# Down projection: nine seven-product tiles in both column pairs, their sums regrouped, two loads moved

## The reference, cut to what matters

```python
def _swiglu(x, w_gate, w_up, w_down):
    return (jax.nn.silu(x @ w_gate) * (x @ w_up)) @ w_down

def reference(x, ...):
    m = _dsa_mixer(x, *mix_p)
    x = _layer_norm(alpha * x + m, ln1_g, ln1_b)
    x = _layer_norm(alpha * x + _swiglu(x, w_gate, w_up, w_down), ln2_g, ln2_b)
    return x
```

## Time and profile before

| | us |
|---|---|
| median of three runs | 916.3 (916.14 to 917.05) |
| the profiled execution | 916.54 |
| its span, first to last instruction | 914.8 |
| outside the span | 1.7 |
| PE busy | 908.9 |
| DVE busy | 774.6 |
| ACT busy | 548.7 |
| POOL busy | 154.3 |

### The profile page before, as it was taken

One profiled execution on the slowest core, in us unless ns is written; L12 is line 12 of the kernel. 1 busy time (PEld: TensorE's weight loads), 2 busy tenths in 40 slices (PEclk: granted clock), 3 DMA queues, 4 the chain that ended last, 5 costly groups with the idle time before them and its releaser, 6 DMA issues.

```text
span 914.8 us, 11657 instructions
## 1 busy us (share of the span) xinstructions
PE 908.9 (99%) x4340; PEld 761.4 (83%) x4340; DVE 774.6 (85%) x963; ACT 548.7 (60%) x748; POOL 154.3 (17%) x119
## 2 busy tenths in 40 slices
PE   9999999999999999999999999999999999999997
PEld 8999988888888888888888888888888888888885
DVE  6778566578799899999999899999989998998677
ACT  5686765345356667666757666675756565466450
POOL 0205540001531214031421214010060000000000
PEclk9999999999999999999999999999999999999999
DMA  9743423574959696969879697978488747365642
GB/s 359 321 177 139 139 92 136 193 312 150 378 165 264 219 310 191 345 182 306 220 250 285 231 317 189 326 206 277 150 306 297 282 184 272 124 247 185 230 138 92
DMA packets 63239, 210.08 MB, mean 230 GB/s; under 512 B 5584, under 2 KB 11728, under 8 KB 51920
## 3 DMA queue, kind: packets, MB, share of 16 engines
q1 hardware_dynamic: 57712, 198.86, 60.6%
q0 software_dynamic: 5472, 10.49, 6.8%
HBM read 199.36 MB, written 9.96 MB: 229 GB/s over the span
## 4 chain that ended last, share of the span: by engine, by line
PE 99%; DVE 0%; ACT 0%; DVEq 0%; issue 0%; ACTq 0%
PE acc L2226 20%; PE acc L2199 18%; PE acc L2181 12%; PE acc L1969 10%; PE tp L2181 9%; PE tp L2199 6%; PE acc L1907 5%; PE tp L2226 5%; PE acc L1828 4%; PE acc L2106 2%; PE tp L2144 2%; PE acc L1941 1%; PE tp L2020 1%; PE tp L1955 1%; PE tp L2033 1%; PE tp L1817 0%
## 5 line engine op out<-in xcount | busy, mean ns | idle before, releaser
L1153 ACT ACTIVATE w_hi<-raw 128x512 fp32r<-128x512 f32 (+1 forms) x164 | 117.7, 761 | 90.9 <-PE acc L2226 70.7
L1576 DVE TENSOR_TENSOR w_lo<-raw,w_hi 128x512 fp32r<-128x512 f32 (+1 forms) x164 | 136.7, 863 | 24.7 <-ACT w_hi L1153 24.1
L2226 PE MATMUL acc<-w_hi,hid_t 128*128 128x512 f32 x480 | 155.5, 389 | 0.0
L2199 PE MATMUL acc<-w_hi,act_t 128*128 128x512 f32 x480 | 154.3, 391 | 0.0
L1507 DVE TENSOR_TENSOR w_lo<-raw,w_hi 128x1024 fp32r<-128x1024 f32 x83 | 104.1, 1256 | 5.4 <-ACT w_hi L1095 5.3
L2199 PEld LDWEIGHTS acc<-w_hi,act_t 128*128 128x128 f32 x480 | 90.1, 188 | 20.7 <-issue 2.1
L1082 ACT ACTIVATE w_hi<-raw_b 128x1024 fp32r<-128x1024 f32 x70 | 74.2, 1060 | 54.2 <-PE acc L2199 31.5
L2226 PEld LDWEIGHTS acc<-w_hi,hid_t 128*128 128x128 f32 x480 | 90.1, 188 | 18.8
L1082 ACT ACTIVATE w_hi<-raw 128x1024 fp32r<-128x1024 f32 x63 | 66.6, 1058 | 48.5 <-PE acc L2199 33.5
L1501 DVE TENSOR_TENSOR w_lo<-raw_b,w_hi 128x1024 fp32r<-128x1024 f32 x70 | 86.9, 1242 | 10.0 <-ACT w_hi L1082 10.0
L2226 PE MATMUL acc<-w_lo,hid_t 128*128 128x512 f32 x240 | 93.4, 389 | 0.0
(11 more groups left out here) (294 smaller groups left out, 1939.8 us busy)
## 6 DMA issues: line engine op xcount, KB each, us to landing
raw<-in_w_pairs SPq DMA_DIRECT2D x116, 512.0 KB, 6.3
raw<-in_w_down SPq DMA_DIRECT2D x44, 1024.0 KB, 5.7
raw_b<-in_w_pairs SPq DMA_DIRECT2D x40, 512.0 KB, 8.0
raw<-in_w_out SPq DMA_DIRECT2D x16, 1024.0 KB, 4.9
raw<-in_w_gu SPq DMA_DIRECT2D x8, 1024.0 KB, 11.4
raw<-in_x_w SPq DMA_DIRECT2D x14, 552.0 KB, 7.4
hid_blocks<-local SPq DMA_DIRECT2D x11, 512.0 KB, 8.5
turned<-hid_blocks SPq DMA_DIRECT2D x44, 128.0 KB, 4.3
```

The lines of the kernel that those rows point to most:

```text
L1153: act.activation(unit_parts(u)[0], block_of(b, block, width), ACT.Copy).then_inc(down_hi_done, 1)
L1576: dve.tensor_tensor(lo_, block_of(b, block, width), hi_, ALU.subtract).then_inc(down_lo_done, 1)
L2199: last = pe.matmul(out[:, t, :], act_t[:, k0 + m, x, t * P:(t + 1) * P], part[:, cols][:, m * GC:(m + 1) * GC], start=False, stop=(end and ...
L2226: last = pe.matmul(bank, lhs(x), part[:, cols * GC:(cols + 1) * GC], start=(first == u and (cols, x) == (0, 0) and part is hi_), stop=(end ...
```

## The change

Both pairs get nine quads. A quad's seven products are put into four units: W1 (blocks B11 and B21, two products, two blocks wide), W2 (t1 and B22, two products, two wide), T2 (t2, one product, one wide) and W3 (t3 and t4, two products, two wide). The order is W1, in most quads a plain unit, W2, a plain unit, T2, W3. The sum t1 is made by an accumulating DMA that POOL issues (`add_down`); t2 is made by DVE right after the low part of W2, and t3 and t4 after the low part of the unit behind W2. A quad's slot is loaded in two transfers of 512 KB, first the half with B12 and B22, which t1 waits for. There are still four slots; a slot is now given to the load whose predecessor ends first (`down_places`). The load of `x1` moves behind the load of slot 9, that of the norm rows behind the load of slot 36; slot 5 comes after `blocks_store`, and slot 6 after `blocks_load`. The low part of the second late tile moves from POOL to DVE (`LATE_LOW`).

```diff
-QUADS_OF = (len(DOWN_QUADS), EARLY_QUADS)
-REST = ((18, 19), (20, 21)), ((14, 15), (16, 17), (18, 19), (20, 21))
+QUAD_UNITS = ((B11, 2, (S_A11, S_A12)), (B12, 2, (S_S1, S_S4)), (B12, 1, (S_S2,)), (B11, 2, (S_S3, S_A22)))
+QUADS_OF = (len(DOWN_QUADS), len(DOWN_QUADS))
+LEAD = ((1,), ())
+BETWEEN = ((3, 5, 7, 9, 11, 13, 15, 17), (1, 3, 5, 7, 9, 11, 13))
+REST = ((18, 19), (20, 21)), ((15, 17), (18, 19), (20, 21))
...
+        extra = len(halves) - quads
+        doubled = {n * quads // extra for n in range(extra)}
+        for q in range(quads):
+            w1, w2, t2, w3 = [(DOWN_QUADS[q], ("quad", q, m)) for m in range(len(QUAD_UNITS))]
+            steps += [w1] + ([halves.pop(0)] if q in doubled else []) + [w2, halves.pop(0), t2, w3]
...
-LAST_TURN = 8
-LAST_HID = 28
-LATE_HIGH = 4
+LAST_TURN = 5
+LAST_HID = 17
+LATE_HIGH = 8
+LATE_LOW = 10
...
+def down_places():
+    held, place, prior = {}, [], []
+    for b in range(len(DOWN_SLOTS)):
+        if b < DOWN_PLACES:
+            at = (b + 2) % RING
+        else:
+            at = min(range(RING), key=lambda n: SLOT_LAST[held[n]])
...
 (load_down)
-                    sp.wait_ge(down_lo_done, SLOT_LAST[b - RING] + 1)
-                sp.dma_start(raw[:, down_slot(b), :], a["w_down"][b]).then_inc(raw_full[down_slot(b)], 16)
+                    sp.wait_ge(down_lo_done, SLOT_LAST[DOWN_PRIOR[b]] + 1)
+                n, src = DOWN_PLACE[b], a["w_down"][b]
+                if b in QUAD_SLOTS:
+                    sp.dma_start(block_of(b, B12, 2), src[:, B12 * GC:(B12 + 2) * GC]).then_inc(right_full_d[n], 16)
+                    sp.dma_start(block_of(b, B11, 2), src[:, B11 * GC:(B11 + 2) * GC]).then_inc(down_full[n], 16)
+                else:
+                    sp.dma_start(block_of(b, 0, 4), src).then_inc(down_full[n], 16)
...
 (the SP queue)
-            sp.wait_ge(ffn_full, TILES)
-            sp.wait_ge(x1_stored, 16)
-            sp.dma_start(x1[:], x1_rows).then_inc(x1_back, 16)
-            for b in range(RING, RING + 2):
+            load_down(RING)
+            blocks_store(PAIRS - 1)
+            load_down(RING + 1)
+            blocks_load(PAIRS - 1)
+            for b in range(RING + 2, len(DOWN_SLOTS)):
                 load_down(b)
-            blocks_store(PAIRS - 1)
-            for b in range(RING + 2, 2 * RING):
-                load_down(b)
-            blocks_load(PAIRS - 1)
-            rows(ln2_rows, 2, ln2_rows_full)
-            for b in range(2 * RING, len(DOWN_SLOTS)):
-                load_down(b)
+                if b == X1_BEHIND:
+                    sp.wait_ge(ffn_full, TILES)
+                    sp.wait_ge(x1_stored, 16)
+                    sp.dma_start(x1[:], x1_rows).then_inc(x1_back, 16)
+                if b == ROWS_BEHIND:
+                    rows(ln2_rows, 2, ln2_rows_full)
...
 (DVE)
+            def quad_t2(u):
+                b = DOWN_UNITS[u][1]
+                dve.wait_ge(down_lo_done, u + 1)
+                dve.tensor_tensor(block_of(b, B12), block_of(b, B12), block_of(b, B22), ALU.add).then_inc(t_done, 1)
+
+            def quad_t34(u):
+                b = DOWN_UNITS[u][1]
+                b11, b21, t2 = (block_of(b, n) for n in (B11, B21, B12))
+                dve.wait_ge(t_done, quad_sums(u) + 1)
+                dve.tensor_tensor(b11, t2, b11, ALU.subtract).then_inc(t_done, 1)
+                dve.tensor_tensor(b21, t2, b21, ALU.add).then_inc(t_done, 1)
...
 (POOL)
+            def add_down(b):
+                n = DOWN_PLACE[b]
+                pool.wait_ge(right_full_d[n], 16 * quad_fill(b))
+                pool.dma_start(block_of(b, B12), a["w_down"][b][:, B11 * GC:(B11 + 1) * GC],
+                               accum_op=ALU.add).then_inc(t1_full_d[n], 16)
+
+            add_down(QUAD_SLOTS[0])
             pool.wait_ge(*used_step(V_OF[PAIRS - 1, "right", P4]))
             pool.wait_ge(ffn_lo, PAIRS - 2)
             late_sums(0)
-            late_low(0)
+            late_low_0()
             pool.wait_ge(late_step, 5)
             late_sums(1)
-            late_low(1)
+            for b in QUAD_SLOTS[1:]:
+                add_down(b)
```

More of the change, by code:

```diff
@@ L208, in down_plan @@
     for pair in range(DOWN_PAIRS):
[L209 to L216, removed]
+        quads = QUADS_OF[pair]
+        steps = [(tile, ("plain", tile, col)) for tile in LEAD[pair] for col in range(2)]
+        halves = [(tile, ("plain", tile, col)) for tile in BETWEEN[pair] for col in range(2)]
+        extra = len(halves) - quads
[3 more added lines that the diff above has]
+            steps += [w1] + ([halves.pop(0)] if q in doubled else []) + [w2, halves.pop(0), t2, w3]
         held = {}
-        for tile, kind, x, y in steps:
+        for tile, what in steps:
             if tile not in held:
-                held[tile] = slot(pair, "both", (tile,))
-            place = (Q_BLOCK[y], 1) if kind == "product" else (2 * y, 2)
-            units.append((pair, held[tile]) + place + ((kind, x, y),))
+                held[tile] = slot(pair, "both" if what[0] == "plain" else "quad", (tile,))
+            place = QUAD_UNITS[what[2]][:2] if what[0] == "quad" else (2 * what[2], 2)
+            units.append((pair, held[tile]) + place + (what,))
         for col in range(2):
@@ L260 @@
                        and DOWN_SLOTS[unit[1]][1] == f"n{col + 1}") for pair in range(DOWN_PAIRS) for col in range(2))
-LAST_PRODUCT = tuple(max(u for u, unit in enumerate(DOWN_UNITS) if unit[0] == pair and unit[4][0] == "product")
+LAST_PRODUCT = tuple(max(u for u, unit in enumerate(DOWN_UNITS) if unit[0] == pair and unit[4][0] == "quad")
                      for pair in range(DOWN_PAIRS))
-QUAD_FIRST = tuple(min(u for u, unit in enumerate(DOWN_UNITS) if unit[4][:2] == ("product", q))
+QUAD_FIRST = tuple(min(u for u, unit in enumerate(DOWN_UNITS) if unit[4][:2] == ("quad", q))
                    for q in range(len(DOWN_QUADS)))
@@ L266 @@
 FIRST_N2 = tuple(min(u for u, unit in enumerate(DOWN_UNITS) if unit[0] == 1 and unit[4][0] == kind and unit[4][2] == n)
-                 for kind, n in (("product", 3), ("plain", 1)))
+                 for kind, n in (("quad", 1), ("plain", 1)))
+DOWN_PLACES = RING
+def down_places():
[5 more added lines that the diff above has]
+            at = min(range(RING), key=lambda n: SLOT_LAST[held[n]])
+        place.append(at)
+        prior.append(held.get(at))
+        held[at] = b
+    return place, prior
+DOWN_PLACE, DOWN_PRIOR = down_places()
+X1_BEHIND = 9
+ROWS_BEHIND = len(DOWN_SLOTS) - 8
+QUAD_SLOTS = tuple(b for b in range(len(DOWN_SLOTS)) if DOWN_SLOTS[b][1] == "quad")
 AFTER_IN = {R_QIDX: IN_SPLITS - 3, R_QIDX + 1: IN_SPLITS - 2, R_QIDX + 2: IN_SPLITS, R_QIDX + 3: IN_SPLITS}
@@ L603, in banks_of, with quad_fill, quad_sums @@
             return acc[:, 0:2, :] if i // 2 % 2 == 1 else tp[:, 0:2, :]
-        def down_slot(b):
-            return (b + 2) % RING
         def down_fill(b):
-            return fills(R_FFN + RING + down_slot(b)) + b // RING + 1
+            return sum(DOWN_PLACE[c] == DOWN_PLACE[b] for c in range(b + 1))
+        def quad_fill(b):
+            return sum(DOWN_PLACE[c] == DOWN_PLACE[b] for c in QUAD_SLOTS if c <= b)
+        def quad_sums(u):
+            pair, _, _, _, (_, q, _) = DOWN_UNITS[u]
+            return QUAD_SUMS * (sum(QUADS_OF[:pair]) + q)
         def used_unit(u):
@@ L626, in block_of @@
         def block_of(b, block, width=1):
-            return raw[:, down_slot(b), block * GC:(block + width) * GC]
+            return raw[:, DOWN_PLACE[b], block * GC:(block + width) * GC]
         def split_place(v):
@@ L2226, in multiply @@
                     last = pe.matmul(bank, lhs(x), part[:, cols * GC:(cols + 1) * GC],
-                                     start=(first == u and (cols, x) == (0, 0) and part is hi_),
+                                     start=(first == u and opens and x == 0 and part is hi_),
                                      stop=(end and x == 1), skip_group_check=(first != u))
```

86 lines of the change are left out of this document (48 added, 38 removed).

## The result

The changed kernel takes 919.65 us (median of 9) where the kernel before takes 916.73 beside it: ratio 1.0029, 95% interval 1.0020 to 1.0037. It is 2.9 us slower, outside the range of the prediction, which had put 0.24 on slower and 0.12 on what happened. One profiled execution among the experiments (b12_quiet) ran at a granted clock of 0.655 and is not read; the ratios are of undisturbed executions alone.

A forecast was written before the change was run, and what follows sets the result against it. PE was taken as the bound, with matmuls back to back in Down. Terms -1.36 (matmuls) + 0.95 (distance) + 0.4 (start) + 0.1 (norm rows) = +0.1 us on 916.3 gave 916.4 us, range 914.8 to 918.9.

The forecast's parts named there:

- t1 by DMA ... cost 0: Tightest quad slots in Down: 3.9 us load plus 6.2 us accumulate fits 10.36 us with 0.26 in hand; cost 0.
- slot 30's 6.46 us: Landing time left for t1 in the tightest slots, 10.36 - 3.9; each microsecond beyond it was to cost three.
- The rival: t1 lands late, W2 waits in slots 17, 30, 37; decides at 7.0 us landing, 922.5 us at 8.5; chance 0.12.
- the row of 10.6 us: Landing of the second of two accumulating transfers, twice as large as t1, which met more loads; the first took 6.2.
- the DMA share of 0.55: Busy share of the DMA engines in Down before the change, taken as t1's surroundings for the 6.2 us bound.
- The norm rows: Issued behind slot 36, with slot 37's first half behind them; its t1 0 to 0.6 us late, 0.1 taken.
- my tight slots: Slots 17, 30 and 37, with 12.92 us in the plan from place free to W2's start, 10.36 after W2's parts.
- The distance ahead: Ring of blocks: plain units 28, 76, 98, 109 keep only 2.72 us; they and W3 stall 0.24 us a quad, 0.95 total.
- The start: Start of Down: slot 6 waits behind the store, which lands after 6.7 us; unit 15 late by 0.4 us.
- The saved matmuls: Two tiles of pair 1 go from 24 to 21 matmuls, 1008 to 1002 in Down: 1.36 us less.
- DVE's room: DVE needs 8.1 us a quad against 10.2 on PE; the free two microseconds cover three moved edits at no cost.
- Both rules that the prediction weighed: Skill rules: VectorE holding shared ports shuts out GpSimd's descriptor writes; t1's transfer fits 2.6 us (2.0 plus bytes at 436 GB/s).

The follow-up runs named there:

- b12_quiet: Changed kernel with the block t1 is added into loaded first by itself in each quad's slot, norm rows behind slot 25: 919.24 us, ratio 1.0028.
- as_is: The changed kernel itself, no edit, profiled and measured a second time: 919.90 us, ratio 1.0037 to the kernel before.
- left_first: Changed kernel with the left half of each quad's slot loaded before the right half that t1 is added into: 922.03 us, ratio 1.0060.
- hold_quiet: Changed kernel with slot 31's load held until slot 30's t1 has landed, norm rows behind slot 25: 916.66 us, ratio 0.9999.
- t1_on_dve: Changed kernel with t1 added by VectorE ahead of W1's low part, no accumulating DMA in Down: 918.31 us, ratio 1.0017.
- rows_early: Changed kernel with only the norm rows moved, behind slot 20 instead of slot 36: 917.56 us, ratio 1.0012.
- spread_quiet: Changed kernel with pair 1's second plain units in quads 1, 3, 4, 5, 8, norm rows behind slot 25: 916.86 us, ratio 1.0006.

## Why the prediction was wrong

**The step that failed** is "t1 by DMA ... cost 0". I took 6.2 us as the bound above for t1's landing, from the first of two accumulating transfers of 512 KB in gate and up, because "half as many bytes move among 1 MB of other loads". The runs show that bytes are not what sets it: the 256 KB landed in 4.2 to 4.9 us with little beside them, 5 to 6.5 mostly, 6.8 to 7.8 at slot 30 beside the load of slot 31, 8.2 to 9.7 at slot 31 behind it, and 8.6 to 12.2 beside 2 MB of x1 or norm rows issued before it. For W2 itself, slot 30's 6.46 us were right: 7.2 us of landing, 0.75 over, cost 0.66 + 0.11 there. The plain unit behind W2 then lost 0.48 us more, and this the prediction left out. Its low part stands on VectorE behind W2's and t2, so it needs t1 about half a microsecond sooner than W2 does. Every late W2 brought this loss with it, 0.46 to 0.58 us whether W2 was 0.25 us late (as_is, slot 30) or 1.94 (left_first, slot 35). In hold_quiet it shows alone: slot 37's W2 is in time, and the plain unit behind it, 109, is 0.36 us late. The chain leads from slot 37's t1 to that unit:

```profile
858.71 6.10 DMA raw<-in_w_down
...
869.07 3.03 PE acc L2291 x12
```

**The rival was there, at 0.12**, with its deciding point at a landing of 7.0 us. For it spoke the row of 10.6 us, which I set aside as "twice as large". Two errors kept its chance small. I took the DMA share of 0.55 as the load that t1 would meet; over the same stretch it was 0.61 in t1_on_dve, which has no such transfers, and 0.76 with them. And I took a mean over a stretch, where slot 30's and slot 31's places come free 2.3 us apart.

**The norm rows** were costed at 0.1 us, at slot 37. SP's queue was followed rightly, and the wrong neighbour chosen: slot 37's halves, which SP issues next, were late by nothing. Slot 35's t1, which is issued on POOL's queue 1.6 us after the rows, took 10.4 us. Slot 35 was not among my tight slots (16.32 - 2.56 = 13.76 us, against 12.92 - 2.56 = 10.36); 5.15 + 0.35 + 10.42 = 15.9 us was too much even so. Cost 1.7 us in the profile; rows_early took 2.3 from as_is.

**Slot 17**, the third that I named, was in time (its t1 took 6.0 us, beside 1 MB that was issued 0.57 us ahead of it).

**The distance ahead**: predicted 0.95 us in four quads; found 0.16 each, 0.65 together, at the units named and at their W3. Mechanism right, a little over-sized.

**The start**: predicted 0.4 at unit 15; nothing. The store of the hidden tiles landed in 2.9 us, not 6.7; there is no gap above 0.02 us before 728. From after's transfers of Down (count, KB, us to landing), with the two whose landing grew:

```profile
raw<-in_w_down POOLq DMA_DIRECT2D x17, 256.0 KB, 6.0
x<-out SPq DMA_DIRECT2D x1, 2048.0 KB, 11.0
ln_rows<-in_ln_rows SPq DMA_DIRECT2D x2, 1024.0 KB, 10.7
...
hid_blocks<-local SPq DMA_DIRECT2D x1, 512.0 KB, 2.9
```

**The saved matmuls** are there (PE's instructions fell from 4340 to 4334), and **DVE's room** for the moved low parts and residuals was as computed in the changed kernel; t1_on_dve and spread_quiet show how little more would have been too much. The tail is 0.04 us longer.

The sum as measured in the profile of after: -1.36, + 2.96 for t1 in slots 30 and 35 with the latter's W3 (1.25 + 1.48 + 0.23), + 0.79 at the short distance and slot 30's W3, + 0 at the start, + 0.04 for the tail, and 0.4 that is spread over Down in steps too small to place: 2.8 us, the difference of the medians being 2.9.

**Both rules that the prediction weighed.** POOL's issue never stuck: 18 of them took 859 ns each (page of after, L1856) beside a VectorE busy for 0.83 of the time, so nothing of that kind cost here. What the Trainium skill says of GpSimd kept from writing descriptors (SBUF — State Buffer, SBUF: two separate sides) is tied to VectorE operations in a two-port mode, a condition that the prediction left out; no run here shows in which mode VectorE's operations ran. The row of the issues:

```profile
L1856 POOL DMA_DIRECT2D raw<-in_w_down x18 | 15.5, 859 | 219.0 <-DMA raw<-in_w_down 219.0
```

The Trainium skill's fit for such a transfer (DMA: Bandwidth & Descriptors, Anatomy of one DMA — SWDGE (gpsimd) path), 2.6 us by estimate, is under every landing seen here, 4.2 to 12.2 us; the measurement decides.

**Waiting or sharing.** The DMA packets in the traces show that slot 30's t1 did both. POOL's packets are those of q0, SP's those of q1 (packets, MB, share of the DMA engines). In the 3.14 us behind t1's issue, rows_early (822.36 to 825.50, first line) moved none of q0, and hold_quiet (822.47 to 825.61, second line) most of t1:

```profile
q1 hardware_dynamic: 248, 0.88, 93.6%
...
q0 software_dynamic: 106, 0.21, 44.9%
```

The first packet of t1 started 3.2 us behind the issue in rows_early and 1.6 us in hold_quiet; from there to the landing it took 4.15 and 2.70 us. So about half of the 3.1 us is a later start, and half is a slower passage among the packets of slot 31's load.

What stays open: why slot 31's load, 1 MB in two halves, costs slot 30's t1 that much, when slots 17 and 28 of the changed kernel had 1 MB issued 0.6 us ahead of t1 and landed in 6.0 us; and why some executions wait near 260 us.

## What to carry to other kernels

A transfer that must be waited for twice in a row (a load, then one that adds to it) is to be costed slot by slot against what the other queues issue in the same few microseconds, not by a mean share of the DMA engines or by its own bytes. Move a large, unhurried load to where such a transfer, on any queue and not only the load's own, has time to spare: with the norm rows behind slot 25, slot 24's t1 took 10.3 us in hold_quiet and nothing waited for it. And when an edit that saves a little takes the slack from a few places, take the part of the saving that leaves the slack (eight quads with two plain units each, not nine).

## What was not expected of the hardware

The landing of the same 256 KB accumulating transfer ran from 4.2 to 12.2 us with the traffic around it, and issuing it 0.3 us earlier behind its slot's load did not bring its end forward (11.58 us behind that load, and 11.43). One megabyte taken from beside it shortened it from 7.4 to 4.2 us, about half of that by an earlier first packet.
